# RWKV chunks of two decoder layers on one core: dense states, products on alternate halves, values' products ahead, norm by row tile

## Chip, cores and metric

One core of a Trainium2 chip runs the whole program. The metric is the device time of one execution in microseconds. TensorE's clock has two levels here, 2.4 GHz (granted clock 1.00 in the profile) and 1.2 GHz (0.50).

## Reference

Two stacks of two layers work on 256 tokens of 1024 features in float32. The change touches the second stack, whose layers `l` = 0, 1 each start with

```python
cols_a, cols_b, gate_a, gate_b = split_cols(h @ w_in[l], IN_SIZES)
y_a, v_first = rwkv7_branch(cols_a, ...)      # 8 heads of 64
y_b = dsa_branch(cols_b, ...)
merged = sigmoid(gate_a) * (y_a @ w_branch_a[l]) + sigmoid(gate_b) * (y_b @ w_branch_b[l])
x = x + merged @ w_out[l]
```

Within `rwkv7_branch` the state of a head, 64x64, runs over the tokens, and the output is normed by head:

```python
def step(state, inp):
    r_t, w_t, k_t, v_t, a_t, b_t = inp
    sa = jnp.einsum('bhvk,bhk->bhv', state, a_t)
    state = (state * w_t[:, :, None, :] + sa[..., None] * b_t[:, :, None, :]
             + v_t[..., None] * k_t[:, :, None, :])
    return state, jnp.einsum('bhvk,bhk->bhv', state, r_t)
...
y = (y - mean) * lax.rsqrt(var + RWKV_LNX_EPS)              # mean, var over the 64 of a head
y = y * lnx_g + lnx_b + bonus * v                           # bonus: one number per token and head
return y * g
```

## The kernel before

The program is written engine by engine, each with its own order of instructions; semaphores hand work over. A row tile `m` is 128 tokens (two of them). Weights come in pieces of 1 MB through a ring of five slots, issued by SyncE in the order in which they are planned; a piece waits until the one five places earlier has been used.

The recurrence is done in four chunks `c` of 64 tokens, `m, half = divmod(c, 2)`: a chunk lies in one half of the 128 partitions of its row tile. `solve_tensor` inverts the chunks' triangular matrices by doubling (`products`, L1893, 64x64 matmuls that alternate between the two halves of the partitions), and ends with VectorE's eviction of `("Y", l, g, 5)` into `self.solve`. Before it, L1884 forms the pair products in all four quarters (rows by columns) of the array.

Then `chunks_tensor` (all its products have line L1985) does for each chunk:
- the right side: 8 products of `packed[..., 1, :]` with the values, and for `c` > 0 4 products with the carried state, 128 rows deep: the state of two heads is one 128x128 block with zeros outside its two diagonal blocks (`zeros_gpsimd` writes the zeros);
- VectorE copies it to `self.rhs` (L2043);
- the output's first part: 8 products with the values, 4 with the carried state;
- the new state: 4 products of keys with values (64 rows deep, 128 wide), each followed for `c` > 0 by a product of the identity with the carried state, 128x128;
- `self.solve` times the right side, 8 products; ScalarE copies the result to `self.sa` (L2032), for which TensorE waits;
- 4 products of `self.bh` with it into the state, which VectorE scales by the decay (L2049, one instruction for each half), and 8 products into the output, which ScalarE copies (L2034).

PSUM has eight banks of 512 columns; right side, sa, output and state alternate between two banks each.

After the chunks come, on TensorE: `gate_tensor(pe, l, 1, 1)`, the fourth gate projection (16 matmuls of 128x128 on 512 columns); `turn_tensor(ya_turn)`, eight transposes of the normed `y`; `merge_tensor`, branch products a, b for columns 0 to 511, then a, b for 512 to 1023. On VectorE: `finish_vector` (L2060 to L2086, the norm over both row tiles at once, with a power on GpSimd, L506), the copy of the turned `y`, and `merge_vector`.

A float32 matmul leaves two records in the trace.

## Time and profile before

| | us |
|---|---|
| median of 3 runs | 3280.16 (3278.95 to 3289.49) |
| the profiled execution | 3287.36 |
| its span | 3285.6 |
| TensorE busy | 3075.7 (94% of the span) |
| VectorE busy | 1504.1 (46%) |
| ScalarE busy | 1029.3 (31%) |
| GpSimd busy | 108.3 (3%) |

The page gives the busy share of the engines and the granted clock in 40 slices, so a slice is 82 us. Views of the trace give single stretches in microseconds from the start of the span. In them PE is TensorE, PEld its weight load, DVE VectorE, ACT ScalarE, POOL GpSimd, SP SyncE, and what stands in brackets is the idle time before an instruction and what ended it.

### The profile page before, as it was taken

How to read it: one execution, taken by the hardware profiler on the slowest of the kernel's cores; microseconds unless marked ns; L12 is line 12 of the kernel's file. 1: busy time of each engine (PE TensorE's matmuls, PEld its weight loads, DVE VectorE, ACT ScalarE, POOL GpSimd, SP SyncE). 2: the span in 40 equal slices, each digit the busy share in tenths (PEclk: the TensorE clock that was granted, in tenths of full speed). 3: DMA queues.
4: the chain of work that ended last, by engine and by line, in shares of the span. 5: the costliest groups of instructions: out<-in, count | busy, mean ns of one | idle time of the engine just before them, and what ended most of it. 6: DMA issues, size and time to landing. Idle time of an engine off the chain costs nothing.

```text
span 3285.6 us, 35140 instructions
## 1 busy us (share of the span) xinstructions
PE 3075.7 (94%) x15248; PEld 2287.2 (70%) x15248; DVE 1504.1 (46%) x1739; ACT 1029.3 (31%) x1200; POOL 108.3 (3%) x105
## 2 busy tenths in 40 slices
PE   7996999999999999898799999978999999999999
PEld 6874567878785768744574588536746888888887
DVE  3455235454545154425723544267235444454444
ACT  3442124434342234203101343131013334334343
POOL 0001000000011000000100000001000000000000
PEclk9998999999999999998869999989699999999999
DMA  7541335556541535433204355432043455555554
GB/s 263 179 164 52 114 119 183 175 177 216 182 162 52 172 135 193 158 128 120 66 26 142 128 192 184 150 103 66 26 143 127 163 192 187 184 175 183 189 183 137
DMA packets 226582, 483.73 MB, mean 147 GB/s; under 512 B 11678, under 2 KB 45086, under 8 KB 225982
## 3 DMA queue, kind: packets, MB, share of 16 engines
q1 hardware_dynamic: 226048, 477.83, 43.1%
q10 hardware_dynamic: 380, 3.66, 0.4%
q8 instruction: 120, 1.97, 0.3%
q14 instruction: 34, 0.28, 0.0%
HBM read 476.75 MB, written 2.95 MB: 146 GB/s over the span
## 4 chain that ended last, share of the span: by engine, by line
PE 82%; DVE 9%; DMA 4%; ACT 2%; issue 1%; POOL 1%; SPq 0%; ACTq 0%; DVEq 0%; POOLq 0%
PE psum L354 19%; PE psum L351 17%; PE psum L353 17%; PE psum L352 17%; PE psum L1985 3%; PE psum L1893 2%; PE psum L715 2%; PE psum L690 1%; PE psum L472 1%; PE psum L557 1%; DMA weight_ring<-in_moe_wd 1%; PE psum L700 1%; ACT weight_high_halves L340 1%; DVE stage_area_halves L463 1%; DMA weight_ring<-in_ffn_w_gate 1%
## 5 line engine op out<-in xcount | busy, mean ns | idle before, releaser
L346 DVE TENSOR_TENSOR weight_ring_low_halves<-weight_ring,weight_high_halves 128x2048 fp32r<-128x2048 f32 (+1 forms) x346 | 741.7, 2151 | 879.7 <-ACT weight_high_halves L340 879.7
L351 PE MATMUL psum<-weight_high_halves,stage_area_halves 128*128 128x512 f32 (+2 forms) x2616 | 1008.1, 385 | 50.4 <-DVE stage_area_halves L463 36.0
L353 PE MATMUL psum<-weight_high_halves,stage_area_halves 128*128 128x512 f32 (+2 forms) x2616 | 998.2, 382 | 0.0
L352 PE MATMUL psum<-weight_ring_low_halves,stage_area_halves 128*128 128x512 f32 (+2 forms) x2616 | 997.6, 381 | 0.0
L340 ACT ACTIVATE weight_high_halves<-weight_ring 128x2048 fp32r<-128x2048 f32 (+1 forms) x346 | 622.4, 1806 | 794.3 <-PE psum L353 374.6
L354 PE MATMUL psum<-weight_ring,stage_area 128*128 128x512 f32 (+2 forms) x1600 | 671.4, 580 | 9.3 <-issue 6.7
L351 PEld LDWEIGHTS psum<-weight_high_halves,stage_area_halves 128*128 128x128 f32 x2616 | 495.3, 189 | 150.5 <-DVE stage_area_halves L463 26.3
L353 PEld LDWEIGHTS psum<-weight_high_halves,stage_area_halves 128*128 128x128 f32 x2616 | 494.9, 189 | 98.9
L352 PEld LDWEIGHTS psum<-weight_ring_low_halves,stage_area_halves 128*128 128x128 f32 x2616 | 494.4, 189 | 93.1
L354 PEld LDWEIGHTS psum<-weight_ring,stage_area 128*128 128x128 f32 x1600 | 303.6, 192 | 360.7 <-issue 355.6
L453 ACT ACTIVATE stage_area<-psum 128x512 f32<-128x512 f32 (+2 forms) x126 | 72.0, 579 | 608.9 <-PE psum L354 359.6
L460 ACT ACTIVATE stage_area_halves<-psum 128x512 fp32r<-128x512 f32 (+2 forms) x148 | 78.0, 571 | 218.3 <-PE psum L557 137.9
L506 POOL TENSOR_TENSOR small<-small,constants 128x1 f32<-128x1 f32 (+5 forms) x45 | 61.5, 1367 | 2272.0 <-DVE small L858 1213.3
L463 DVE TENSOR_TENSOR stage_area_halves<-psum,stage_area_halves 128x512 fp32r<-128x512 f32 (+2 forms) x148 | 90.4, 650 | 84.2 <-ACT stage_area_halves L460 83.1
L1985 PE MATMUL psum<-stage_area 64*64 64x64 f32 (+2 forms) x704 | 102.1, 332 | 7.1 <-ACT stage_area L2032 5.4
L690 PE MATMUL psum<-stage_area 64*128 64x256 f32 (+1 forms) x288 | 83.0, 436 | 25.2 <-DVE stage_area L745 14.3
L454 DVE COPY stage_area<-psum 128x512 f32<-128x512 f32 (+1 forms) x42 | 28.5, 678 | 165.7 <-PE psum L472 165.4
L1985 PEld LDWEIGHTS psum<-stage_area 64*64 64x64 f32 (+2 forms) x704 | 88.5, 219 | 19.4 <-issue 10.8
L615 ACT ACTIVATE stage_area<-psum 128x512 f32<-128x512 f32 (+2 forms) x108 | 59.6, 555 | 122.4 <-PE psum L353 122.3
L690 PEld LDWEIGHTS psum<-stage_area 64*128 64x128 f32 (+1 forms) x288 | 52.3, 207 | 53.1 <-issue 23.8
L472 PE MATMUL psum<-constants,stage_area 128*128 128x128 f32 x272 | 39.1, 302 | 50.8 <-ACT stage_area L1736 23.7
L715 PE MATMUL psum<-stage_area 128*64 128x256 f32 (+1 forms) x288 | 81.2, 420 | 0.0
(227 smaller groups left out, 1958.4 us busy)
## 6 DMA issues: line engine op xcount, KB each, us to landing
weight_ring<-in_ffn_w_down SPq DMA_DIRECT2D x44, 1024.0 KB, 5.0
weight_ring<-in_ffn_w_gate SPq DMA_DIRECT2D x40, 1024.0 KB, 5.2
weight_ring<-in_ffn_w_up SPq DMA_DIRECT2D x40, 1024.0 KB, 5.2
weight_ring<-in_moe_wd SPq DMA_DIRECT2D x40, 1024.0 KB, 4.9
weight_ring<-in_w_in SPq DMA_DIRECT2D x36, 1024.0 KB, 4.9
weight_ring<-in_moe_wg SPq DMA_DIRECT2D x32, 1024.0 KB, 5.2
weight_ring<-in_moe_wu SPq DMA_DIRECT2D x32, 1024.0 KB, 5.3
weight_ring<-in_mem_w_kv SPq DMA_DIRECT2D x16, 1024.0 KB, 5.1
```

What stands on the lines that cost most here:

```text
L340: act.raw.activation(self.high_half(name), self.in_slot(name), ACT.Copy).then_inc(*act.mark("high_halves", ("high", name)))
L346: v.raw.tensor_tensor(self.low_half(name), self.in_slot(name), self.high_half(name), ALU.subtract).then_inc(*v.mark("low_halves", ("halves ...
L351: pe.raw.matmul(out, a[1], w[0], start=start, stop=False)
L352: pe.raw.matmul(out, a[0], w[1], start=False, stop=False)
L353: return pe.raw.matmul(out, a[0], w[0], start=False, stop=stop)
L354: return pe.raw.matmul(out, a, w, start=start, stop=stop)
L453: return eng.raw.activation(dst, src, ACT.Copy)
L460: eng.raw.activation(dst[0], src, ACT.Copy).then_inc(*eng.mark("high_half_taken", (name, "high")))
L463: eng.raw.tensor_tensor(dst[1], src, dst[0], ALU.subtract).then_inc(*self.drained(eng, bank, full, name))
L690: mm = pe.raw.matmul(net.ps[:, bank, m * S:(m + 1) * S], h["q"](j, m), h["k"](j), start=(j == 0), stop=(j == h["nk"] - 1))
L715: mm = pe.raw.matmul(net.ps[p0:p0 + rows, bank, ct * S:(ct + 1) * S], h["v"](part, kt), net.pT[:, i % 2, kt, :], start=(kt == 0), stop=(kt ...
L1985: return pe.raw.matmul(net.ps[out_rows, bank, at], lhsT, rhs, start=start, stop=stop, skip_group_check=True)
```

## The change

- The states are dense: 64 columns for each head, two heads on the two halves of the partitions. A product with a carried state is 64 rows deep, eight instead of four, alternating between the heads of a pair (`e`). The zeroing on GpSimd goes. The identity product is one, on 256 columns.
- Even and odd heads' right sides and outputs lie in two banks each (0, 1 and 4, 5), with both row tiles in one bank; VectorE copies the even ones and ScalarE the odd ones. sa has bank 2, the state bank 3.
- The products of the values for all four chunks, and the state's for chunk 0, stand ahead of the wait for the solve's end.
- Two terms of the norm's end, `y_gain` = g x lnx_g and `y_bias` = (bonus x v + lnx_b) x g, are made by GpSimd; VectorE norms row tile by row tile, with two instructions at the end in place of five.
- The order after the fourth gate is b branch for both column halves, the turn of `y`, then the a branch row tile by row tile; the branch weights are loaded in the order b, b, a, a.

The removed lines of `chunks_tensor`, `finish_vector` and the merge are in the functions printed above; lines left out are marked.

```diff
-        self.state = [net.part(9216, 4, P), net.part(9728, 4, P)]
+        self.state = [net.part(9216, 4, CH), net.part(9728, 4, CH)]
+        self.y_gain, self.y_bias = (net.ax_buf[:, at:at + D].rearrange("p (m n) -> p m n", m=MT) for at in (0, D))
...
-            st["merge"] = []
-            for nb in range(2):
-                c0 = nb * BANK
...
+            branch = {}
+            for j in (1, 0):
+                for nb in range(2):
+                    w = ins[f"w_branch_{'ab'[j]}_2"][l]
+                    branch[nb, j] = net.plan_proj(f"branch{l}{'ab'[j]}{nb}", w[:, nb * BANK:(nb + 1) * BANK], [(0, BANK)], 4)
+            st["merge"] = [(branch[nb, 0], branch[nb, 1]) for nb in range(2)]
...
-    def zeros_gpsimd(self, pool, l):
-
...
     def chunks_tensor(self, pe, l):
-        pe.wait_ge(*pe.at(("Y", l, 0, 5), ("Y", l, 1, 5), ("zeroed", l)))
+        half_rows = [slice(0, CH), slice(CH, P)]
+        RHS, SA, STATE, Y = (0, 1), 2, 3, (4, 5)
+
+        def rhs_at(rows, e, m, i):
+            return net.ps[rows, RHS[e], m * S + i * CH:m * S + i * CH + CH]
+
+        def y_at(rows, m, h):
+            at = m * S + h // 2 * CH
+            return net.ps[rows, Y[h % 2], at:at + CH]
+
+        def state_at(e, c, i):
+            at = (c % 2) * S + i * CH
+            return net.ps[half_rows[e], STATE, at:at + CH]
+
+        def mm(out, lhsT, rhs, start=False, stop=False):
+            return pe.raw.matmul(out, lhsT, rhs, start=start, stop=stop, skip_group_check=True)
+
+        def rhs_values(m):
+            for i in range(4):
+                for e in range(2):
+                    h = 2 * i + e
+                    for rows in half_rows:
+                        x = mm(rhs_at(rows, e, m, i), self.packed[rows, 8 * m + h, 1, :], self.v[rows, m, h * CH:h * CH + CH], m == 0 and i == 0)
+                    if m == 1 and i == 3:
+                        x.then_inc(*net.full(pe, RHS[e], ("rhs", l, 0, e)))
+
+        def y_values(m):
+            for h in range(8):
+                for rows in half_rows:
+                    mm(y_at(rows, m, h), self.packed[rows, 8 * m + h, 2, :], self.v[rows, m, h * CH:h * CH + CH], m == 0 and h < 2)
+
+        def state_values(c):
+            m, half = divmod(c, 2)
+            rows = half_rows[half]
+            for i in range(4):
+                for e in range(2):
+                    h = 2 * i + e
+                    mm(state_at(e, c, i), self.k[rows, m, h * CH:h * CH + CH], self.v[rows, m, h * CH:h * CH + CH], i == 0)
+
+        for bank in RHS:
+            pe.wait_ge(*net.free(bank))
+        rhs_values(0)
+        rhs_values(1)
+        pe.wait_ge(*net.free(STATE))
+        state_values(0)
+        for bank in Y:
+            pe.wait_ge(*net.free(bank))
+        y_values(0)
+        y_values(1)
+        pe.wait_ge(*pe.at(("Y", l, 0, 5), ("Y", l, 1, 5)))
         for c in range(4):
             m, half = divmod(c, 2)
...
+            rows, state = half_rows[half], self.state[c % 2]
+            tokens = [slice(part * P + CH * half, part * P + CH * half + CH) for part in range(2)]
             if c:
                 pe.wait_ge(*pe.at(("state", l, c)))
...
+                for i in range(4):
+                    for e in range(2):
+                        x = mm(rhs_at(rows, e, m, i), self.arT[half_rows[e], i, m, tokens[0]], state[half_rows[e], i, :])
+                        if i == 3:
+                            x.then_inc(*net.full(pe, RHS[e], ("rhs", l, c, e)))
+                if c < 3:
+                    state_values(c)
+                    mm(net.ps[:, STATE, (c % 2) * S:(c % 2) * S + S], net.ident, state.rearrange("p i d -> p (i d)"))
+                for i in range(4):
+                    for e in range(2):
+                        if c == 2 and i == 0:
+                            pe.wait_ge(*net.free(Y[e]))
+                        mm(y_at(rows, m, 2 * i + e), self.arT[half_rows[e], i, m, tokens[1]], state[half_rows[e], i, :])
+            pe.wait_ge(*net.free(SA))
+            for e in range(2):
+                pe.wait_ge(*pe.at(("rhs_kept", l, c, e)))
+                for i in range(4):
+                    h = 2 * i + e
+                    x = mm(net.ps[rows, SA, h * CH:h * CH + CH], self.solve[rows, 8 * m + h, :], self.rhs[rows, half, h * CH:h * CH + CH], True, True)
+            x.then_inc(*net.full(pe, SA, ("sa", l, c)))
+            pe.wait_ge(*pe.at(("sa_kept", l, c)))
+            if c < 3:
+                for i in range(4):
+                    for e in range(2):
+                        h = 2 * i + e
+                        x = mm(state_at(e, c, i), self.bh[rows, m, h * CH:h * CH + CH], self.sa[rows, half, h * CH:h * CH + CH], False, True)
+                x.then_inc(*net.full(pe, STATE, ("new_state", l, c)))
             for h in range(8):
...
+                x = mm(y_at(rows, m, h), self.packed[rows, 8 * m + h, 0, :], self.sa[rows, half, h * CH:h * CH + CH], False, True)
+                if half and h >= 6:
+                    x.then_inc(*net.full(pe, Y[h % 2], ("y", l, m, h % 2)))
+
+    def rhs_keep(self, eng, l, c, e):
+        m, half = divmod(c, 2)
+        rows = slice(CH * half, CH * half + CH)
+        dst = self.rhs[rows, half, :].rearrange("p (i e d) -> p i e d", i=4, e=2)[:, :, e, :]
+        src = self.net.ps[rows, e, m * S:m * S + S].rearrange("p (i d) -> p i d", i=4)
+        return self.net.copy(eng, dst, src)
+
+    def y_keep(self, eng, m, e):
+        dst = self.y[:, m, :].rearrange("p (i e d) -> p i e d", i=4, e=2)[:, :, e, :]
+        src = self.net.ps[:, 4 + e, m * S:m * S + S].rearrange("p (i d) -> p i d", i=4)
+        return self.net.copy(eng, dst, src)
...
+            self.rhs_keep(act, l, c, 1).then_inc(*net.drained(act, 1, ("rhs", l, c, 1), ("rhs_kept", l, c, 1)))
...
+            if half:
+                act.wait_ge(*act.at(("y", l, m, 1)))
+                self.y_keep(act, m, 1).then_inc(*net.drained(act, 5, ("y", l, m, 1), ("y_kept", l, m, 1)))
...
             if c < 3:
...
+                src = net.ps[:, 3, (c % 2) * S:(c % 2) * S + S].rearrange("p (i d) -> p i d", i=4)
+                v.raw.tensor_tensor(self.state[(c + 1) % 2], src, widen(self.decay_end[:, :, c], 2, CH), ALU.mult).then_inc(
+                    *net.drained(v, 3, ("new_state", l, c), ("state", l, c + 1)))
+            if c == 1:
+                v.wait_ge(*v.at(("y", l, 0, 0)))
+                self.y_keep(v, 0, 0).then_inc(*net.drained(v, 4, ("y", l, 0, 0), ("y_kept", l, 0, 0)))
...
+    def finish_gpsimd(self, pool, l):
+
+        pool.wait_ge(*pool.at(("Y", l, 1, 5), ("rhs", l, 0, 1), ("g", l, 0), ("g", l, 1), ("loaded", ("vec", l, 7))))
+        row = lambda j: widen(self.vec[:, j, :], 1, MT)
+        by_head = lambda ap: ap.rearrange("p (h d) -> p h d", d=HD)
+        pool.raw.tensor_tensor(self.y_gain, self.g, row(6), ALU.mult)
+        for m in range(MT):
+            inst = pool.raw.tensor_tensor(by_head(self.y_bias[:, m, :]), by_head(self.v[:, m, :]), widen(self.bonus[:, m, :], 2, HD), ALU.mult)
+        inst.then_inc(*pool.step())
+        pool.wait_ge(*pool.last)
+        pool.raw.tensor_tensor(self.y_bias, self.y_bias, row(7), ALU.add).then_inc(*pool.step())
+        pool.wait_ge(*pool.last)
+        pool.raw.tensor_tensor(self.y_bias, self.y_bias, self.g, ALU.mult).then_inc(*pool.mark("finish_terms", ("finish_terms", l)))
...
     def finish_vector(self, v, l):
...
+        for m in range(MT):
+            y, tmp = self.y[:, m, :], self.at[:, m, :]
...
+            if m == 1:
+                v.wait_ge(*v.at(("y", l, 1, 0)))
+                self.y_keep(v, 1, 0).then_inc(*self.net.drained(v, 4, ("y", l, 1, 0), ("y_kept", l, 1, 0)))
+            v.wait_ge(*v.at(("y_kept", l, m, 0), ("y_kept", l, m, 1)))
+            v.raw.tensor_reduce(mean, heads(y), AX, ALU.add).then_inc(*v.step())
...
+            v.raw.tensor_scalar(var, var, 1.0 / HD, LNX_EPS, ALU.mult, ALU.add).then_inc(*v.mark("variance_ready", ("var", ("lnx", l, m))))
+            v.wait_ge(*v.at(("rstd", ("lnx", l, m))))
+            v.raw.tensor_tensor(heads(y), heads(y), widen(rstd, 2, HD), ALU.mult).then_inc(*v.step())
+            v.wait_ge(*v.last)
+            v.wait_ge(*v.at(("finish_terms", l)))
+            v.raw.tensor_tensor(y, y, self.y_gain[:, m, :], ALU.mult).then_inc(*v.step())
+            v.wait_ge(*v.last)
+            v.raw.tensor_tensor(y, y, self.y_bias[:, m, :], ALU.add).then_inc(*v.mark("rwkv_done", ("ya", l, m)))
...
     def merge_tensor(self, pe, l):
         net = self.net
...
+        for nb in range(2):
+            net.proj_tensor(pe, self.layers[l]["merge"][nb][1], lambda k, m: self.ybT[:, k, m * P:(m + 1) * P], lambda b, m: (6, 2)[nb] + m)
+        net.turn_tensor(pe, self.ya_turn(l))
+        for m in range(MT):
+            for nb in range(2):
+                tag, bank = self.layers[l]["merge"][nb][0]["tag"], (4, 0)[nb] + m
+                pe.wait_ge(*net.free(bank))
+                pe.wait_ge(*pe.at(("yaT", l, m)))
+                w = net.weights(pe, (tag, 0, 0))
+                for k in range(4):
+                    mm = net.product(pe, net.ps[:, bank, :], self.yaT[:, k, m * P:(m + 1) * P], at_k(w, k), k == 0, k == 3)
+                used = [("used", (tag, 0, 0))] if m == MT - 1 else []
+                mm.then_inc(*net.full(pe, bank, (tag, "full", 0, m), *used))
...
     def merge_vector(self, v, l):
         net = self.net
...
+        for nb in range(2):
+            tag, cols = self.layers[l]["merge"][nb][1]["tag"], slice(nb * BANK, (nb + 1) * BANK)
             for m in range(MT):
+                gb, bank = self.gate[1][:, m, cols], (6, 2)[nb] + m
+                v.wait_ge(*v.at((tag, "full", 0, m), ("gate", l, nb, 1, m)))
+                v.raw.tensor_tensor(gb, net.ps[:, bank, :], gb, ALU.mult).then_inc(*net.drained(v, bank, (tag, "full", 0, m), ("gb", l, nb, m)))
+        for m in range(MT):
+            for nb in range(2):
+                tag, cols, bank = self.layers[l]["merge"][nb][0]["tag"], slice(nb * BANK, (nb + 1) * BANK), (4, 0)[nb] + m
                 out = self.merged[:, m, cols]
+                v.wait_ge(*v.at((tag, "full", 0, m), ("gate", l, nb, 0, m)))
+                v.raw.tensor_tensor(out, net.ps[:, bank, :], self.gate[0][:, m, cols], ALU.mult).then_inc(*net.drained(v, bank, (tag, "full", 0, m), ("ga", l, nb, m)))
                 v.wait_ge(*v.at(("gb", l, nb, m), ("ga", l, nb, m)))
-                v.raw.tensor_tensor(out, out, gb, ALU.add).then_inc(*v.mark("branches_merged", *([("merged", l, m)] if nb == 1 else []), *([("groups_done", l)] if nb == 1 and m == 1 else [])))
+                v.raw.tensor_tensor(out, out, self.gate[1][:, m, cols], ALU.add).then_inc(*v.mark(
+                    "branches_merged", *([("merged", l, m)] if nb == 1 else []), *([("groups_done", l)] if nb == 1 and m == 1 else [])))
...
             self.gate_tensor(pe, l, 1, 1)
-            net.turn_tensor(pe, self.ya_turn(l))
             self.merge_tensor(pe, l)
...
             self.solve_gpsimd(pool, l)
-            self.zeros_gpsimd(pool, l)
-            rstd(("lnx", l), 16, 16)
+            self.finish_gpsimd(pool, l)
+            for m in range(MT):
+                rstd(("lnx", l, m), 16 + 8 * m, 8)
```

## Rows read from the trace of the kernel before

**Rows 1.** The page: granted clock of TensorE in 40 slices, in tenths.
```profile
PEclk9998999999999999998869999989699999999999
```

**Rows 2.** The chain that ended last, around the chunks: start, us, what.
```profile
1644.64 4.22 PE psum L1985 x56
1649.52 18.39 PE psum L1985 x104
1668.58 18.69 PE psum L1985 x104
...
1703.47 16.15 PE psum L354 x32
```

**Rows 3.** Windows: stretch, us, busy time by engine, granted clock, DMA share, GB/s.
```profile
1630.00:1644.00 14.00, 13.80 (x466) 13.66 (x462) 10.07 (x16) 0.00 (x0) 0.00 (x0) 1.00 0.02 4
...
1654.00:1660.00 6.00, 6.00 (x37) 5.24 (x36) 0.69 (x1) 0.00 (x0) 0.00 (x0) 0.50 0.00 0
1643.60:1703.40 59.80, 56.23 (x376) 48.17 (x370) 5.98 (x11) 4.14 (x7) 0.00 (x0) 0.55 0.00 1
2299.35:2359.46 60.11, 56.55 (x376) 48.48 (x371) 5.98 (x11) 4.14 (x7) 0.00 (x0) 0.55 0.00 1
...
1703.40:1719.40 16.00, 16.00 (x33) 6.83 (x32) 12.58 (x13) 1.19 (x2) 3.28 (x1) 0.86 0.13 38
```

**Rows 4.** Timeline of TensorE: start, us, line, tile rows*columns, moving operand, records.
```profile
1607.42 1.98 PE L1884 MATMUL psum<-stage_area 64*64 64x128 f32 x64 [0.78 <-ACT stage_area L453]
...
1641.69 1.10 PE L1893 MATMUL psum<-stage_area 64*64 64x64 f32 x32
1642.65 1.15 PE L1893 MATMUL psum<-scaled_residual 64*64 64x64 f32 x32
...
1644.64 2.05 PE L1985 MATMUL psum<-stage_area 64*64 64x64 f32 x32 [0.84 <-issue]
...
1660.87 0.79 PE L1985 MATMUL psum<-stage_area,constants 128*128 128x128 f32 x2
1661.59 0.79 PE L1985 MATMUL psum<-stage_area 64*128 64x128 f32 x2
...
1665.93 1.97 PE L1985 MATMUL psum<-stage_area 64*64 64x64 f32 x16
...
1720.98 27.70 PE L354 MATMUL psum<-weight_ring,stage_area 128*128 128x512 f32 x64 [0.46 <-issue]
```

**Rows 5.** Timeline of all engines: the hand-overs of the solve's end and chunk 0.
```profile
1641.90 0.69 DVE L1939 TENSOR_TENSOR scaled_residual<-psum,constants 128x512 f32<-128x512 f32 x1 [0.32 <-PE psum L1893]
...
1643.85 0.69 DVE L1951 TENSOR_TENSOR stage_area<-psum,scaled_residual 128x512 f32<-128x512 f32 x1 [0.32 <-PE psum L1893]
...
1644.64 4.20 PE L1985 MATMUL psum<-stage_area 64*64 64x64 f32 x56 [0.84 <-issue]
...
1648.88 0.59 ACT L2032 ACTIVATE stage_area<-psum 64x512 f32<-64x512 f32 x1 [41.60 <-PE psum L1985]
1649.52 1.47 PEld L1985 LDWEIGHTS psum<-stage_area 64*128 64x128 f32 x8 [0.82 <-ACT stage_area L2032]
...
1651.33 0.86 DVE L2049 TENSOR_TENSOR stage_area<-psum,small 64x256 f32<-64x256 f32 x2 [4.79 <-PE psum L1985]
```

**Rows 6.** The norm's end: timeline at the turn, then groups by shape (busy, mean ns).
```profile
1719.42 0.86 PEld L472 LDWEIGHTS psum<-constants,stage_area 128*128 128x128 f32 x8 [0.63 <-DVE stage_area L2086]
...
L2073 DVE TENSOR_TENSOR stage_area<-stage_area,small 128x512 f32<-128x512 f32 x2 | 1.3, 693 | 0.0
...
L506 POOL TENSOR_TENSOR small<-small,constants 128x8 f32<-128x8 f32 x4 | 6.6, 1646 | 52.5 <-DVE small L1517 52.5
```

**Rows 7.** Groups of POOL by shape, two-input operations on wide operands.
```profile
L1958 POOL TENSOR_TENSOR stage_area<-stage_area,constants 128x512 f32<-128x512 f32 x2 | 2.5, 1272 | 48.3 <-DVE stage_area L1928 48.3
...
L893 POOL TENSOR_TENSOR stage_area<-stage_area,constants 128x640 f32<-128x640 f32 x1 | 2.1, 2103 | 0.0
```

**Rows 8.** Timeline of SyncE: issues of branch weights before and in the fourth gate.
```profile
1603.18 0.37 SPq L310 DMA_DIRECT2D weight_ring<-in_w_branch_a  x1
1716.22 0.37 SPq L310 DMA_DIRECT2D weight_ring<-in_w_branch_b  x1
```

129 lines of the change are left out of this document (18 added, 111 removed).

## The prediction

> **What bounds the kernel now.** I read the page first, then the chain that ended last in order of time, then windows, then timelines. The clock row of the page [rows 1] stands near full speed except around slices 20 and 28, the chunk stages of layers 0 and 1. The chain [rows 2] runs there on TensorE's L1985 products alone, from 1644.64 to the gate projection at 1703.4, so TensorE sets the end. The windows [rows 3] say why the stage is long: from the last product of the solve to the gate it takes 59.8 us in layer 0 and 60.11 us in layer 1, TensorE busy for 56 of them at a mean granted clock of 0.55; 1654 to 1660 has it busy without a break at 0.50, the 1.2 GHz level. The solve just before, also of 64x64 products, holds 1.00 (2.4 GHz). The difference is in the form: the solve alternates between the two halves of the partitions, the chunk stage gives one half after another.
>
> The timelines [rows 4] give prices. A product is two records. At full clock:
> - Alternate halves: 32 records start every 0.96 us (1641.69, 1642.65), so 0.12 us per two products, 0.48 per eight.
> - One half: 32 records in 2.05 less a tail of 0.22, so 0.118 per product, 0.945 per eight.
> - All four quarters of the array: L1884, whose moving operand is 128 wide, has 64 records in 1.98 us, about 0.028 per record. One after another, a record twice as wide would take twice 0.059; two at a time would give 0.059, and it's half of that. So products in the same rows but other columns overlap too.
>
> At the low clock eight products in one half take 1.97 less a tail of 0.2, 1.77 us (1665.93). There the values' and identity products alternate every 0.72 us (1660.87, 1661.59). A dense record of 512 columns takes 27.70 / 64 = 0.43 us at full clock, so a product of 128 columns (two records) takes 0.22, and 0.43 at the low clock: about 0.29 is lost at each change between 64x128 and 128x128 tiles.
>
> **The change, part by part.** Counts per layer.
>
> *Values ahead.* 32 right-side, 8 state and 32 output products of values no longer wait for the solve's last eviction: 36 pairs x 0.12 = 4.3 us, and they start at once where 0.84 us of idle stood before 1644.64 [rows 5]. VectorE's last eviction (1643.85, 0.69) lies under them, and so do the first right-side copies.
>
> *Chunks.* Hand-overs [rows 5]: from the last solve-times-right-side product to the first product that reads ScalarE's copy 0.84 us is lost (the group of 56 ends at 1648.84, its last record began 0.22 before and would be followed 0.06 later; the next begins at 1649.52), 0.59 of it the copy. It stays in each chunk. VectorE starts 0.21 us after a last product is issued (1641.90 against the group whose successor starts at 1641.69), works 0.43 on 256 columns, and TensorE follows 0.10 later: 0.75 to 0.8.
> - Chunk 0: two groups in one half 1.89, one pair group 0.48, hand-over 0.84: 3.2 us. The state's scaling now takes one instruction of 256 columns (0.43) in place of two (0.86), and hides under the 0.945 us of output products.
> - Chunks 1 and 2: four pair groups 1.92 (carried state to right side, values to state, carried state to output, bh to state), two one-half groups 1.89, hand-over 0.84. One identity product of 256 columns takes 2 x 0.22 and two changes of tile form. No row shows such a change at full clock; its bounds are 0 and the low clock's 0.58 for both, and I take half, 0.3. Sum 5.4 us each, in place of 19.1 from hand-over to hand-over (1649.52 to 1668.58) [rows 2]. The split right-side copies (0.43 on VectorE, under 0.59 on ScalarE) and the output copy for which chunk 2 waits lie under 1.7 us of products.
> - Chunk 3: two pair groups 0.96, one-half groups 1.89, hand-over 0.84, and here only 0.48 covers the 0.76 of the right-side copies, so 0.28 is late: 4.0 us.
>
> Sum 4.3 + 3.2 + 10.8 + 4.0 = 22.3. Some 20 group starts whose weights aren't ahead add 0 to 0.05 each (the 0.96 already has one in 32 records); I take 0.7: **23.0 us**, bounds 21.7 (neither they nor the changes of form cost anything) and 24 (1.0, and the changes at 0.58). Gain 36.8 and 37.1 us.
>
> This takes 2.4 GHz throughout. It rests on rows: the new stage opens with 4.3 us of pairs, as in the solve; afterwards each chunk is thin around the hand-over, so it's also the weakest assumption.
>
> *Gate and merge.* From the gate's start to the first merge projection 17.58 us pass now (1703.40 to 1720.98): 0.86 mean clock over the gate [rows 3], 0.63 us of waiting for the norm [rows 6], then the turn, 1.5 with its copy (1719.42 to 1720.98) [rows 4, 6]. At full clock the gate's 32 records are half of the 27.70 row less its tail, 13.8 us; then the b branch's 32 run without waiting, 13.8, which is moved and not new, then the turn. So 17.6 becomes 15.3, **2.3 us** less per layer. The merge's last projection is still followed by one multiply and one add before its turn; the turn into bank 1 waits for the multiply, but the row tile 1 group already waits for the add, so that is hidden.
>
> *Norm by row tile.* Each tile has eight VectorE instructions of 512 columns (0.69 [rows 6]), two small ones and a POOL power of 8 columns (1.65): 7.5 us, the first tile starting before chunk 3 ends. Both are done 12 us after the stage; the turn needs them after 27.6 us (gate and b branch). If that cover were gone the 12 us would be paid. The copies of b's products into the gates come behind the turn on VectorE (4 x 0.69), but they hold banks 6, 7, 2, 3, which nobody needs until the merged turn.
>
> *POOL.* Four zeroings go; five tensor operations come, eight times 512 columns: 8 x 1.27 = 10.2 us by L1958 [rows 7], or 13.5 by the slower L893. They start 2.4 us into the stage and are wanted about 24 us in: hidden.
>
> *SP.* The branch pieces come as b, b, a, a. Three are loaded in the solve, the fourth once the gate has read its first piece, three quarters through (1603.18, 1716.22) [rows 8]; a's second is first read 18 us after the gate. Out's pieces follow b, b and a's first: b's come when the first two came, a's first about 4 us later than the old third, and the piece that waits for it is read 20 us later still. Cost nothing; its cover gone, one weight landing.
>
> **The sum.** 36.8 + 37.1 + 2 x 2.3 = 78.5 us off the profiled execution's own 3287.36 (its span 3285.6 and 1.8 around it): 3208.9. That execution stands 7.2 us above the runs' median of 3280.16, so the median is predicted at 3201.7, rounded to **3202**.
>
> **A rule weighed.** The row 1654 to 1660 has TensorE busy without a break and at half clock. The Trainium skill, TensorE: Matmul & The Clock Gate, "Loop structure matters more than you think", says that back-to-back matmuls stay warm; this trace disagrees for products in one half. By that rule alone the new stage stays at full clock, which is the sum above; by the row it may not, which is the first rival.
>
> **Rivals.**
> 1. *The clock falls inside the chunks.* For: the mean of 0.55 [rows 3] is 6 us at 1.00 and the rest at 0.50, so it fell in the first hand-over, after some 28 products mostly in one half; chunk 0 has as thin a stretch. Against: pairs precede and follow. At the low clock groups cost 0.96 and 1.77, the identity product 1.44: chunks 1 and 2 take 9.7 each, chunk 3 6.3, with 4.3 of values and 4.2 (between 3.2 and 5.3) for chunk 0 before: 34.2, and the gate's 2.3 goes too. A layer then gives 25.6 in place of 39.1: one layer 3216, both 3229.
> 2. *Halves don't overlap in the new tiles.* The carried-state and state products use the same columns or the same rows. 13 groups x 0.46 = 6.0 us per layer: 3214. L1884's four at once speak against.
> 3. *Two halves in one bank go singly.* The 64 values' products of prelude pairs would take 3.7 us more per layer: 3209. The solve's pairs share a bank and overlap [rows 4], so 1 in 100. The Trainium skill, TensorEngine Tiling, "Gotcha 1: PSUM Pressure", says that different row tiles cannot access the same PSUM bank at once; by that rule, 3209; the trace disagrees.
> 4. *Slower: POOL's terms come late.* VectorE stands in order at the wait for them, and ya, its turn and the drains stand behind. The turn is due 50 us in, and 9 us of norm follow the wait, so it starts to cost once POOL needs over 38 us for its 10.2, and decides once it passes 38 + 39 = 77 us, seven times the row; the slowest comparable row gives 13.5. Then over 3280; 1 in 100.
>
> **Chances.** Full clock through the chunks 0.62; rival 1 0.24 (one layer 0.14, both 0.10); rival 2 0.08; rival 3 0.01; rival 4 and anything else that eats it 0.02; no measurable change 0.01; the rest, 0.02, small extra waits. The likeliest one's own range is 3195 to 3209: twice the stage's bounds (3199 to 3204), widened by some 5 us to each side, half of what the runs of before lie apart (3278.95 to 3289.49). **3194 to 3231** reaches over rivals 1 to 3 and leaves out about 0.1. A change within 0.3%, 10 us, can't be told from none: faster 0.97, same 0.01, slower 0.02.
>
> **What would show it.** The granted clock at 1.00 from the solve through the gate; the stage 23 us; 64x64 records a few ns apart in pairs in the carried-state and state groups; one 128x128 product of 256 columns in chunks 1 and 2; ScalarE's sa copy followed by 0.1 us to TensorE; no wait before the ya turn; POOL's five operations over by mid-stage. Wrong: 0.50 in the stage, single spacing of 0.058 in the pair groups, a wait on VectorE's rhs or state instruction longer than 0.3 us, or TensorE idle at the turn.

## The result, and the profile after

The median of four runs fell from 3281.05 to **3206.95 us** (3196.75 to 3211.01), a ratio of 0.9765 with a 95% interval of 0.9736 to 0.9794; 3202 was forecast, within 3194 to 3231. The profiled execution took 3208.12 us with a span of 3206.3; its sum had been put at 3208.9. Of the page, the clock row answers to [rows 1]; the dents at the two chunk stages are gone, those that remain are elsewhere.

```profile
PEclk9998999999999999989899999988999999999999
```

The chain that ended last, around the chunks of layer 0 (start, us, what), answers to [rows 2]:

```profile
1640.99 5.14 PE psum L1980 x159
...
1646.15 0.60 ACT stage_area L2073
...
1646.80 4.56 PE psum L1980 x96
...
1651.38 0.60 ACT stage_area L2073
...
1657.24 1.91 PE psum L1980 x46
...
1659.17 0.44 DVE stage_area L454
...
1660.83 0.60 ACT stage_area L2073
...
1662.62 27.66 PE psum L354 x64
```

TensorE still holds the chain, but ScalarE's copy of sa now appears in it once per chunk, and VectorE's right-side copy once, in chunk 3. A chunk is 5.2 us long where one was 19.

In what follows the *stage* is the time from the solve's last product to the first one of the fourth gate, and the *merged turn* is the transpose of the merged branches, the first work that needs all of the merge. The windows of the stage in both layers, then the gate (columns as in [rows 3]; the five busy times are PE, PEld, DVE, ACT and POOL):

```profile
1640.77:1662.55 21.78, 19.01 (x461) 17.46 (x457) 6.84 (x14) 4.21 (x9) 9.05 (x5) 1.00 0.01 3
2258.41:2280.19 21.78, 19.01 (x460) 17.46 (x456) 6.83 (x14) 4.21 (x9) 9.05 (x5) 1.00 0.01 3
1662.55:1676.35 13.80, 13.80 (x34) 6.18 (x33) 7.98 (x15) 0.98 (x2) 3.29 (x2) 1.00 0.14 39
```

59.83 and 60.13 us became 21.78 twice, and the granted clock of both stages is 1.00 where it was 0.55. The timeline of the stage (engine, line, tile, moving operand, records):

```profile
1640.82 5.29 PE L1980 MATMUL psum<-stage_area 64*64 64x64 f32 x160
1641.04 0.69 DVE L1952 TENSOR_TENSOR stage_area<-psum,scaled_residual 128x512 f32<-128x512 f32 x1 [0.32 <-PE psum L1894]
1642.79 0.42 DVE L454 COPY stage_area<-psum 64x256 f32<-64x256 f32 x1 [1.06 <-PE psum L1980]
...
1643.00 2.35 POOL L2098 TENSOR_TENSOR scaled_residual<-stage_area 128x1024 f32<-128x1024 f32 x1 [29.57 <-PE psum L1980]
...
1646.15 0.59 ACT L2073 ACTIVATE stage_area<-psum 64x512 f32<-64x512 f32 x1 [2.87 <-PE psum L1980]
...
1646.80 2.37 PE L1980 MATMUL psum<-stage_area 64*64 64x64 f32 x64 [0.68 <-ACT stage_area L2073]
...
1649.09 0.70 PE L1980 MATMUL psum<-stage_area,constants 128*128 128x256 f32 x2
...
1649.72 1.61 PE L1980 MATMUL psum<-stage_area 64*64 64x64 f32 x32
1649.86 2.35 POOL L2105 TENSOR_TENSOR scaled_residual<-scaled_residual,stage_area 128x1024 f32<-128x1024 f32 x1
...
1652.02 2.37 PE L1980 MATMUL psum<-stage_area 64*64 64x64 f32 x64 [0.68 <-ACT stage_area L2073]
...
1659.65 1.00 PEld L1980 LDWEIGHTS psum<-stage_area 64*64 64x64 f32 x16 [0.18 <-DVE stage_area L454]
...
1661.47 1.14 PE L1980 MATMUL psum<-stage_area 64*64 64x64 f32 x16 [0.68 <-ACT stage_area L2073]
```

The values' products start 0.05 us behind the solve, with VectorE's last eviction lying beside them. From one hand-over to the next it is 5.22 us (1646.80, 1652.02), and the only idle time of TensorE left is 0.68 us before ScalarE's copy has landed, four times; in chunk 3 its weight loads also wait 0.18 us for the right-side copy. POOL works from 1643.00 to 1652.2.

At the turn (answers to [rows 6]):

```profile
1690.12 1.04 PE L472 MATMUL psum<-constants,stage_area 128*128 128x128 f32 x8
1691.55 1.95 PE L354 MATMUL psum<-weight_ring,stage_area 128*128 128x512 f32 x4 [0.39 <-issue]
```

The transposes follow the b branch without waiting; VectorE's norm had ended at 1674.45, 11.9 us after the stage.

Where the 79.24 us between the two profiled executions lie: 38.05 and 38.35 in the stages; 2.81 ahead of the first one, in code that is the same (1643.58 and 1640.77 from the start, with 129.7 and 126.3 us of low clock, of which the 3.4 us less can make 1.7 at most); and 0.03 in all the rest. The 2.24 us per layer at the merge don't show in the end, to which I come back.

### The profile page after: what moved, and what is told of

Its sections match the earlier page's. It is cut to its first block, busy times and chain, and to the rows that moved or that the text cites. A ratio compares the mean times of both kernels' runs of the same rounds, so it can differ in the third digit from the quotient of the medians.

```text
span 3206.3 us, 35492 instructions
## 1 busy us (share of the span) xinstructions
PE 2995.8 (93%) x15416; PEld 2224.0 (69%) x15416; DVE 1495.7 (47%) x1747; ACT 1029.0 (32%) x1204; POOL 124.1 (4%) x109
## 4 chain that ended last, share of the span: by engine, by line
PE 83%; DVE 9%; DMA 4%; ACT 2%; issue 1%; SPq 0%; POOL 0%; ACTq 0%; DVEq 0%; POOLq 0%
PE psum L354 20%; PE psum L351 18%; PE psum L353 17%; PE psum L352 17%; PE psum L1894 2%; PE psum L715 2%; PE psum L690 1%; PE psum L472 1%; DMA weight_ring<-in_moe_wd 1%; PE psum L1980 1%; PE psum L557 1%; PE psum L700 1%; ACT weight_high_halves L340 1%; DVE stage_area_halves L463 1%; DMA weight_ring<-in_ffn_w_gate 1%
## 5 line engine op out<-in xcount | busy, mean ns | idle before, releaser
L453 ACT ACTIVATE stage_area<-psum 128x512 f32<-128x512 f32 (+3 forms) x138 | 76.4, 561 | 699.5 <-PE psum L354 360.0
L454 DVE COPY stage_area<-psum 128x512 f32<-128x512 f32 (+2 forms) x54 | 33.5, 621 | 203.4 <-PE psum L472 196.9
L690 PE MATMUL psum<-stage_area 64*128 64x256 f32 (+1 forms) x288 | 82.9, 435 | 25.2 <-DVE stage_area L745 14.3
L615 ACT ACTIVATE stage_area<-psum 128x512 f32<-128x512 f32 (+2 forms) x108 | 59.5, 554 | 120.9 <-PE psum L353 120.8
L690 PEld LDWEIGHTS psum<-stage_area 64*128 64x128 f32 (+1 forms) x288 | 52.1, 207 | 52.9 <-issue 23.7
L472 PEld LDWEIGHTS psum<-constants,stage_area 128*128 128x128 f32 x272 | 35.0, 156 | 61.2 <-ACT stage_area L1737 25.6
L351 PE MATMUL psum<-stage_area_halves,weight_ring_low_halves 128*128 128x256 f32 x256 | 72.8, 285 | 4.7 <-DVE stage_area_halves L463 4.7
```

The lines of the kernel that those rows point to most:

```text
L351: pe.raw.matmul(out, a[1], w[0], start=start, stop=False)
L453: return eng.raw.activation(dst, src, ACT.Copy)
L472: mm = pe.raw.transpose(self.ps[:, g["bank"], i * P:(i + 1) * P], block, self.ident)
L690: mm = pe.raw.matmul(net.ps[:, bank, m * S:(m + 1) * S], h["q"](j, m), h["k"](j), start=(j == 0), stop=(j == h["nk"] - 1))
```

## Experiments

### Which part holds the clock

**All groups one half after another.** Same products and waits, the halves no longer alternate.

```diff
-            for i in range(4):
-                for e in range(2):
-                    ...
-                    for rows in half_rows:
-                        x = mm(rhs_at(rows, e, m, i), ...)
+            for rows in half_rows:
+                for i, e in ((i, e) for i in range(4) for e in range(2)):
+                        x = mm(rhs_at(rows, e, m, i), ...)
...
-                for i in range(4):
-                    for e in range(2):
+                for e in range(2):
+                    for i in range(4):
```

(the first hunk in both sets of values' products, the second in the state, carried-state and bh groups)

> The changed kernel with each group's two halves given one after the other: the same products and the same waits, but no product has one of the other half for its neighbour. My theory (the alternation of halves holds the granted clock and gives the overlap): the first 4 to 6 us still run at 1.00, then the clock falls to 0.50 as it did in the kernel before, and the stage takes 50 to 56 us in place of 21.8 (all at the low clock: 72 values' products x 0.221 = 15.9, chunk 0 6.2, chunks 1 and 2 12.9 each, chunk 3 8.2), so some 60 us more in all, 3270. Rival (what holds the clock is that the products stand close together, with few waits): clock 1.00 throughout, only the overlap is lost, 36 pairs x 0.116 = 4.2 and eleven chunk groups x 0.46 = 5.1, the stage 31 us, in all 3225.

3232.49 us, one run. Windows of layer 0 up to the clock's fall and from it to the gate, and of layer 1's stage:

```profile
1640.01:1649.86 9.85, 9.17 (x198) 9.03 (x195) 1.53 (x3) 0.97 (x2) 6.23 (x4) 1.00 0.01 3
1649.86:1676.68 26.82, 24.78 (x266) 22.56 (x263) 5.87 (x14) 3.29 (x7) 4.45 (x3) 0.50 0.01 1
2268.61:2301.15 32.54, 29.82 (x461) 27.88 (x457) 7.40 (x16) 4.26 (x9) 10.70 (x6) 0.75 0.01 2
```

The theory is right in kind and too dark in size: the clock falls to 0.50, but only 9.85 and 16.1 us into the stage, which takes 36.7 and 32.5 us. The rival's clock of 1.00 throughout is out.

**Only the chunks' groups so ordered** (the second hunk alone).

> The changed kernel with the values' products in alternate halves as they are, and only the chunks' groups (first state, carried state to right side and output, values to state, bh to state) given one half after another. With every group so given the clock fell 9.8 and 16.1 us into the stage; with only the values' so given it held. Theory (what loses the clock is a stretch whose products are nearly all in one half, with the hand-overs between): it falls here too, 5 to 10 us into the stage, and the stage takes 28 to 35 us with 12 us or more at 0.50. Rival (the stage's 4.3 us of pairs at its start are enough to hold it): 1.00 throughout and 21.8 + 11 groups x at most 0.46 = 24 to 26.9 us.

3231.82 us, one run:

```profile
1639.15:1652.07 12.92, 11.56 (x280) 10.88 (x276) 1.96 (x4) 1.94 (x4) 9.05 (x5) 1.00 0.01 3
1639.15:1670.10 30.95, 28.23 (x460) 26.29 (x456) 7.39 (x16) 4.26 (x9) 10.70 (x6) 0.71 0.01 2
2265.06:2299.03 33.97, 31.25 (x461) 28.89 (x457) 7.40 (x16) 4.26 (x9) 10.68 (x6) 0.62 0.01 2
```

The fall comes 12.9 and 8.2 us in, for 18.0 and 25.7 us. The alternation in the chunks is worth 9.2 and 12.2 us of stage, most of it clock; the pairs that open the stage don't hold the clock by themselves.

**Only the values' products so ordered** (the first hunk, and the same in `y_values`).

> The changed kernel with only the values' products ahead of the stage given one half after another; the state, carried-state and bh groups stay pairs. If the clock holds: 21.8 + 32 x 0.116 = 25.5 us at 1.00. If it is the one-half order ahead of the chunks that loses the clock (it fell 10 to 16 us into the stage where all groups were so given, and 6 to 7 us in where the values stood in the chunks): low from some 8 to 15 us on, 30 to 37 us.

3201.82 us, one run:

```profile
1634.93:1659.01 24.08, 21.31 (x461) 19.75 (x457) 6.84 (x14) 4.21 (x9) 9.04 (x5) 1.00 0.01 3
```

The clock holds through the stage in both layers (in layer 0 it falls behind it, see below), and the price is 2.30 us, not 3.7: the first group takes 7.59 us in place of 5.29. Its records start 58 ns apart inside a half, but some 6 ns apart for a few records where the order goes from one half to the other, so a short run of eight products is partly overlapped with the next.

**Values' products back in the chunks, in one half.**

```diff
-        rhs_values(0)
-        rhs_values(1)
+        rhs_values(0)                      # chunk 0's half alone
...
-        y_values(0)
-        y_values(1)
+        y_values(0)
...
+            if c < 3:
+                rhs_values(c + 1)
+                y_values(c + 1)
             pe.wait_ge(*net.free(SA))
```

> The changed kernel with the values' products back in the chunks, in one half: only chunk 0's 24 stand ahead, and each chunk gives the right-side and output values' products of the next one (16, in its half) before its own solve products. The other groups stay pairs, the states dense. My theory (the 72 products ahead are paid for only by the overlap they gain; the chunks' pair groups hold the clock): if the clock stays at 1.00 the stage is 21.8 + 32 pairs x 0.116 = 3.7, less 0.3 in chunk 3, whose late right-side copy is now covered: 25.2 us. Rival (a chunk with more one-half products than pairs loses the clock): 0.50 from chunk 0 or 1 on, about 24 one-half and 16 pair products per chunk, the stage 42 to 45 us (29.9 us for the chunks at the low clock's prices, 64 x 0.221 = 14.1 for the values, 1.0 for the first state's).

3239.68 us, one run:

```profile
1639.16:1644.95 5.79, 5.11 (x108) 4.97 (x106) 1.11 (x2) 0.97 (x2) 4.43 (x4) 1.00 0.01 3
1644.95:1674.73 29.78, 27.74 (x356) 25.62 (x356) 6.07 (x13) 3.29 (x7) 4.61 (x2) 0.54 0.01 2
2269.63:2305.71 36.08, 33.36 (x461) 31.00 (x457) 7.18 (x15) 4.26 (x9) 10.35 (x6) 0.59 0.01 2
```

My theory's 25.2 us at full clock is wrong. The rival's forecast holds in kind (a fall 5.8 us into the stage, 6.8 in layer 1), its 42 to 45 us are too many. The same 64 products given one half after another hold the clock when they all stand ahead in one piece, and lose it with 48 of them moved into the chunks: 14 us per layer, of which at most 3.7 are overlap. Why is open. In layer 0 the fall comes 0.13 us behind the first hand-over, before chunk 1, where the stage had given 48 products, all but the 8 of the state in one-half order (4.93 us), and a wait; with all 64 ahead it had given 80, again all but 8 in that order (7.59 us), and the same wait, and held. So what later chunks look like can't have brought this fall, and no run gives the values' products in the chunks and yet in alternate halves.

### How near the stage is to losing it

**Longer hand-overs.** ScalarE copies sa three times, then six times.

```diff
+            for _ in range(2):             # second kernel: range(5)
+                act.raw.activation(self.sa[rows, half, :], net.ps[rows, 2, :], ACT.Copy).then_inc(*act.step())
+                act.wait_ge(*act.last)
             act.raw.activation(self.sa[rows, half, :], net.ps[rows, 2, :], ACT.Copy)...
```

> The changed kernel with ScalarE's copy of the solve products done three times in a row, so that TensorE waits 0.68 + 2 x 0.6 = 1.9 us at each of the four hand-overs in place of 0.68. It asks how near the new stage is to losing the clock by its waits. If waits alone of this size don't matter: 1.00 throughout, the stage 21.8 + 4 x 1.2 = 26.6 us. If the stage stands near the edge: the clock falls to 0.50 in the chunks, over 32 us.

> As the one before, with the copy done six times: TensorE waits 0.68 + 5 x 0.6 = 3.7 us at each hand-over, about as long as the chunk's products take. At 1.00 the stage would be 21.8 + 12 = 33.8 us. I expect the clock to fall here from the first or second hand-over on, as TensorE is idle for nearly half of the time: over 40 us. Rival (waits don't count, only what the products are): 33.8 us at 1.00.

3229.33 and 3261.1 us, one run each. TensorE's timeline in the first kernel:

```profile
1643.67 3.76 PE L1980 MATMUL psum<-stage_area 64*64 64x64 f32 x64 [1.93 <-ACT stage_area L2076]
...
1647.36 1.22 PE L1980 MATMUL psum<-stage_area,constants 128*128 128x256 f32 x2
...
1653.27 4.17 PE L1980 MATMUL psum<-stage_area 64*64 64x64 f32 x64 [1.93 <-ACT stage_area L2076]
```

its windows up to the clock's fall and over the stage:

```profile
1636.40:1644.19 7.79, 5.86 (x185) 5.73 (x181) 1.11 (x2) 2.15 (x4) 5.48 (x4) 1.00 0.02 4
1636.40:1671.87 35.47, 27.75 (x461) 25.45 (x457) 7.18 (x15) 9.01 (x17) 10.50 (x6) 0.66 0.01 2
```

and the stage of the second:

```profile
1651.40:1694.88 43.48, 28.27 (x460) 25.96 (x457) 9.36 (x19) 16.12 (x29) 10.68 (x6) 0.66 0.01 2
```

At waits of 1.93 us in place of 0.68 the clock falls right behind the first one, 7.8 us into the stage (9.4 in layer 1). The waits themselves cost 5.0 us; the stage grows by 13.7 and 12.4, to 35.5 and 34.2. The products and their order are those of the changed kernel, so waits count too, and the stage of the changed kernel stands within 1.25 us per hand-over of the edge. Six copies give 43.5 and 44.4 us, as expected.

Three other profiles bear on the margin. Their stages end at full clock, but the clock falls 0.3 to 0.4 us into the dense products of the gate and stays low for 3.4 us: in layer 0 of the kernel with the values' products in one half after another, in layer 0 of the one begun at the low clock (next), and in layer 1 of the one with the chunks alone (below), whose stage is the changed kernel's. The gate's 13.8 us from its start, first and last of these:

```profile
1659.01:1672.81 13.80, 13.80 (x30) 6.00 (x29) 7.99 (x15) 0.98 (x2) 3.29 (x2) 0.88 0.04 3
2273.87:2287.67 13.80, 13.80 (x30) 6.00 (x29) 11.07 (x13) 0.98 (x2) 3.28 (x1) 0.88 0.05 3
```

In the first two the merged turn comes 1.70 us later for it (44.51 us after the gate's start in place of 42.81). The other layer of each, and both profiles of the changed kernel, have the gate at full clock. As the third of these stages is the changed kernel's, 21.78 us with the same waits, an execution of the changed kernel may pay this too.

**The stage begun at the low clock.**

```diff
+        pe.wait_ge(*pe.at(("paused", l)))
         for bank in RHS:
...
+        for _ in range(8):                 # VectorE, ahead of its part in the chunks
+            inst = v.raw.tensor_reduce(self.hs[:, 0:2], self.v, AX, ALU.add)
...
+        v.raw.tensor_reduce(self.hs[:, 0:2], self.v, AX, ALU.add).then_inc(*v.mark("pause_over", ("paused", l)))
```

> The changed kernel with nine VectorE reductions of 1024 columns (about 10 us) between the solve and the chunks, for which TensorE waits, so that the stage begins at the low clock; it prices the first rival of the prediction. If a stage that begins low stays low, it takes 39.6 us from its first values' product to the gate (values 8.6, chunk 0 5.3, chunks 1 and 2 9.7 each, chunk 3 6.3), and the gate begins low too. If the values' pairs bring the clock back, it is about 8.6 + 17.5 = 26 us, and the values ahead are what warms the stage as well as what holds it.

3237.27 us, one run. Windows from the first values' product on:

```profile
1658.49:1661.65 3.16, 3.11 (x58) 3.12 (x60) 0.00 (x0) 0.00 (x0) 0.00 (x0) 0.50 0.02 5
1661.65:1681.71 20.06, 17.29 (x400) 15.74 (x396) 6.14 (x13) 4.21 (x9) 9.05 (x5) 1.00 0.01 2
2285.59:2309.25 23.66, 20.83 (x453) 19.29 (x453) 6.15 (x13) 4.21 (x9) 9.04 (x5) 0.91 0.01 3
```

3.16 us of pairs bring back 2.4 GHz (4.1 in layer 1), and it then holds to the gate: 23.2 and 23.7 us in place of 21.8. So the stage repairs a start at the low clock for under 2 us, less than the 26 us in all that I gave for this case.

### The tail and the merge

**The merge as before** (chunks and the norm by row tile as changed).

```diff
+            net.turn_tensor(pe, self.ya_turn(l))
             self.merge_tensor(pe, l)       # a, b, a, b again, weights in that order
```

> The changed kernel with the merge as before: ya's turn right behind the fourth gate, then a, b, a, b, and the weight pieces in that order; chunks and the norm by row tile stay. Prediction's reading (the 2.3 us come from the full clock in the gate and from the norm that is over in time, and the new order of the branches is only cover): both norm tiles end 12 us after the stage, under the gate's 13.8, so no wait at the turn, and the merged turn starts 42.9 us after the gate's start, as in the changed kernel (42.81): total the same within 0.1%. Rival (the new order itself saves): the merged turn 45.1 us after the gate's start, total 4.6 us more.

Ratio to before 0.9755 (0.9737 to 0.9772), median 3205.6. The timeline at its turn:

```profile
1672.55 1.04 PE L472 MATMUL psum<-constants,stage_area 128*128 128x128 f32 x8
...
1673.97 2.38 PE L354 MATMUL psum<-weight_ring,stage_area 128*128 128x512 f32 x5 [0.39 <-issue]
```

13.84 us after the gate's start TensorE turns without waiting, and the merged turn starts at 42.81 us, to 0.01 as with the new order. The order of the branches is worth nothing here.

**Chunks alone:** in addition the norm over both row tiles, with the five instructions of its end, as in the kernel before.

> The change's chunk part alone: chunks of the changed kernel, with norm, POOL terms, turn and merge as before. My theory: stage 21.8 us at 1.00; the norm over both tiles ends about 16.0 us after the stage, the gate's 13.8 us end first, and the turn waits 2.2 to 2.9 us, so the merged turn starts 45.1 us after the gate's start. 76.4 us less than before in the two stages. If what the gate and merge gain is given back later anyway (both profiles reach the end of the kernel the same time after the gate), the total equals the changed kernel's; if that was chance, it is 4.5 us (0.14%) longer. Rival (the new tail is what makes the stage short): stage over 23 us.

Ratio 0.977 (0.9745 to 0.9794), median 3212.64.

```profile
1672.62 1.23 DVE L2128 TENSOR_TENSOR stage_area<-stage_area 128x1024 f32<-128x1024 f32 x1
1673.90 0.86 PEld L472 LDWEIGHTS psum<-constants,stage_area 128*128 128x128 f32 x8 [2.64 <-DVE stage_area L2128]
1673.90 1.09 PE L472 MATMUL psum<-constants,stage_area 128*128 128x128 f32 x8 [1.82 <-DVE stage_area L2128]
```

The stage is 21.78 us; the turn waits 1.82 us for the norm and the merged turn starts at 44.91 us, 2.10 later than in the changed kernel and 0.21 earlier than before (45.12). So the gate's full clock by itself buys 0.2 us, because the norm becomes late; the shorter norm buys 2.1 on top of it. Layer 1 confirms it: 3.4 us of its gate ran at 1.2 GHz, and its merged turn starts at 44.91 as well, where with the norm by row tile the same stretch costs 1.70 us. In the total neither can be told: the three kernels' intervals overlap.

### Both kernels once more

> The changed kernel itself, for comparison on the same chip: stage 21.8 us in both layers at 1.00, about 3207. Its time between the gate of layer 0 and the solve's end of layer 1, and behind the gate of layer 1 (595.87 and 926.12 in its first profile, 595.93 and 926.09 before the change) says whether the 2.2 us that the gate and merge gain are always given back in the feed-forward parts (then 596 and 926 again) or whether that was where low-clock stretches fell (then they vary by some us).

Median 3200.74 us (3198.11 to 3203.55), ratio 0.9733 (0.9715 to 0.975), stages 21.78 us.

> The kernel before, profiled once more. Its stages 59.8 and 60.1 us, low for 53 to 54 of them. Behind the gate of layer 1 its first profile took 926.09 us, and seven profiles with new chunks took 924.2 to 927.2 though the merged turn came 2.24 us sooner in six of them. If the feed-forward part takes the gain back (TensorE waits there longer for weights), 926 again; if the first profile was a lucky one, 928 or more.

3284.68 us, one run; stages 60.01 and 58.22 us. The two layers answer differently.

*Layer 0.* From its gate to the end of layer 1's solve the changed kernel took 595.87 us at first and 590.16 now, the kernel before 595.93 and 592.56. In the first profile of the changed kernel a low-clock stretch fell 329.1 us behind the gate, into the end of the feed-forward part, which neither the kernel before nor the second profile has there: 1.9 us of the gain stood before it and nothing behind it. In the second profile the gain of 2.2 us still stands at 355 us behind the gate. Of seven profiles with the new chunks (the changed kernel's two, those with an older tail, with the values' products in one-half order, begun low, and with filled hand-overs) three have that stretch and took 594.0 to 595.9 us, and four have not and took 590.0 to 592.4. Where it falls differs from one execution to the next, and what decides it is not shown.

*Layer 1.* Behind the gate it is 926.12 and 926.05 us with the change, 926.09 before, and 929.33 in its second profile, where a low-clock stretch 162 us behind the gate lasted 10.2 us and not 3.4. Windows of the expert layers, the same distances behind the gate; of before, of before again (second part only), and of the changed kernel:

```profile
2554.16:2919.46 365.30, 362.88 (x1708) 307.58 (x1707) 174.16 (x118) 145.94 (x116) 0.00 (x0) 1.00 0.55 183
2919.46:3281.46 362.00, 358.43 (x1686) 303.17 (x1684) 168.95 (x116) 139.60 (x112) 0.00 (x0) 1.00 0.52 173
```

```profile
2913.54:3275.54 362.00, 358.93 (x1690) 304.12 (x1690) 170.10 (x116) 141.49 (x113) 0.00 (x0) 1.00 0.52 175
```

```profile
2474.89:2840.19 365.30, 361.65 (x1703) 306.69 (x1702) 173.97 (x117) 146.59 (x117) 0.00 (x0) 1.00 0.54 181
2840.19:3202.19 362.00, 356.67 (x1681) 302.21 (x1679) 167.62 (x116) 138.80 (x112) 0.00 (x0) 1.00 0.52 173
```

TensorE is idle there for 5.99 us before and 8.98 with the change (5.92 and 8.30 in the second profiles): arriving 2.24 us sooner, it waits 2.4 to 3.0 us more between the experts' products. It waits for ScalarE's activation, which stands in order behind the splitting of the experts' weights, and that in part waits for their landing; ScalarE's waits for landings grow only from 170.1 to 173.9 us in the first profiles. That the transfers take the gain back is possible and not shown: no run slowed or quickened them, and other profiles don't fit it. Over the same windows five more have 6.7 to 8.4 us of idle time, 7.55 of it in the kernel with the chunks alone, which arrived only 0.2 us sooner; and the kernel with the values' products in one-half order, which has the changed tail and a low-clock stretch of the same 3.4 us, took 924.25 us from layer 1's gate to the end, 1.84 less than before. So the gain was lost in both profiles of the changed kernel, and it need not be.

### Work put into the hand-overs

```diff
         y_values(0)
-        y_values(1)
...
                 if c < 3:
                     state_values(c)
-                    mm(net.ps[:, STATE, (c % 2) * S:(c % 2) * S + S], net.ident, state.rearrange("p i d -> p (i d)"))
...
             x.then_inc(*net.full(pe, SA, ("sa", l, c)))
+            if c == 0:
+                y_values(1)
+            elif c < 3:
+                mm(net.ps[:, STATE, (c % 2) * S:(c % 2) * S + S], net.ident, state.rearrange("p i d -> p (i d)"))
             pe.wait_ge(*pe.at(("sa_kept", l, c)))
```

> The changed kernel with work put into the hand-over around ScalarE's copy of the solve products (0.68 us of TensorE waiting, four times per layer): in chunk 0 the second row tile's 16 output values' products (0.96 us) stand behind the solve products in place of ahead of the stage, in chunks 1 and 2 the identity product (0.70). What stays ahead of the solve products, 0.96 us of pair groups, still covers the right-side copies (0.43 and 0.59, 0.76 with their starts). Theory: three of four waits of 0.68 go, the stage takes 21.78 - 2.04 = 19.7 us at 1.00, 4 us less in all (0.13%), which is within what runs of one kernel differ by. Rival (the identity product behind the solve products puts its change of tile form and its wait for the state's bank onto the path, or the right-side copies are no longer covered): the wait moves to the right-side copies or to bh's products, and the stage stays over 21 us.

```profile
1650.79:1670.13 19.34, 18.51 (x460) 17.23 (x456) 6.84 (x14) 4.21 (x9) 9.06 (x5) 1.00 0.02 3
2264.97:2284.32 19.35, 18.52 (x461) 17.23 (x457) 6.84 (x14) 4.21 (x9) 9.06 (x5) 1.00 0.01 3
```

and the one hand-over of layer 0 at which TensorE still waits, chunk 3's:

```profile
1669.06 1.14 PE L1980 MATMUL psum<-stage_area 64*64 64x64 f32 x16 [0.68 <-ACT stage_area L2075]
```

The stage takes 19.35 us in both layers, 2.43 less than in the changed kernel, a little more than the three waits of 0.68; the chunks are 4.45 us apart instead of 5.22, so a little of the change of tile form (from 64x64 to 128x128 and back) probably goes with the wait. In the total it doesn't show: 3202.79 us (0.9736, 0.9717 to 0.9754) against 3200.74 for the changed kernel on the same chip. It is the shortest stage of all. With one wait of 0.68 left in place of four it should also be the one farthest from the edge found above; no run lengthened its waits to show it.

## Why the prediction was right

*The stage, 23.0 us with bounds 21.7 to 24: measured 21.78 in both layers, close to the lower bound.* Term by term: values and chunk 0 were put at 7.5 us and took 7.45 (6.03 from 1640.77 to 1646.80, then one pair group and one one-half group, 1.42). Chunks 1 and 2: 5.4 each, measured 5.22. The identity product and its two changes of tile form were put at 0.73 and take 0.63 from its start to the next product's, with another 0.09 lost before its start: both changes cost 0.3, as taken from bounds of 0 and 0.58. Chunk 3: 4.0, measured 3.9, its late right-side copy 0.18 and not 0.28. The sa hand-over was 0.84 and is 0.85 by the same reckoning. The term that failed is the 0.7 for some 20 group starts: in sum it measures nothing. By the starts of the single records some do cost (the carried states' output group takes 0.52 us in place of 0.48, and the values-to-state group 0.62 with the 0.09 just named), but a one-half group followed by a pair group is overlapped with it, which the sum had not foreseen: chunk 0's outputs and chunk 1's right side take 1.16 us in place of 1.43. So 0.7 + 0.36 + 0.1 + 0.05 make up the 1.2, with errors that partly cancel.

*2.4 GHz throughout, the weakest assumption: held in all eight stages profiled with the changed chunk code as it is (the changed kernel twice, and the two with an older tail).* The gate held too in seven of the eight. The reason given was the 4.3 us of pairs that open the stage, and that was not it: in one-half order these products hold the clock as well, and as pairs they don't hold it over one-half chunks. That it held was a choice with 0.62 on it and not a derivation. The runs show three conditions, and each one taken away alone lost the clock in both layers of its one profile: pairs within the chunks (9 to 12 us without), the values' products out of the chunks (14 us), short hand-overs (12 to 14 us at 1.93, 5.0 of it the waits themselves). On the rule weighed: the Trainium skill, TensorE: Matmul & The Clock Gate, "Loop structure matters more than you think", says that matmuls issued back to back stay warm and long waits between them cool the engine. The longer hand-overs agree with its second half, with waits of only 1.93 us. With its first half the kernel before disagrees [rows 3], busy 6.00 of 6.00 us at 0.50. And at the same waits of 0.68, one-half order in the chunks alone loses the clock (0.71 and 0.62 over the stage), so how the products lie in the array counts beside how closely they follow each other.

*Rival 1* had 0.24 and didn't happen in the changed kernel; it is what happens in five of the variants. Its price, 34.2 us for the stage, is near what those took (31.0 to 36.7, without the one with six copies), but doesn't come from the same terms: they fell later and hold more waits or less overlap, so the nearness is in part luck. (One layer's price in the total is 3215, not 3216.)

*Rivals 2 and 3:* out. 160 records open the stage in 5.29 us; a carried-state group of eight products starts its records in pairs 6 ns apart. The Trainium skill, TensorEngine Tiling, "Gotcha 1: PSUM Pressure", has different row tiles unable to use one bank at once; the values' pairs write one bank from both halves, at 0.12 us a pair, so the trace disagrees again.

*Gate and merge, 2.3 us per layer: 2.31 measured at the merged turn's start, 2.24 at the first projection behind it,* but the step named two causes as a sum, the gate's clock and the end of the norm's wait, and they aren't independent. The 0.63 us read as waiting for the norm [rows 6] are the weight load's; the turn's products followed the gate's without a visible wait, because the slow gate (16.06 us) ended as late as the norm. So the full clock had 2.25 us to give, and without the shorter norm it gives 0.2. And the gain doesn't reach the end in either profile of the changed kernel that was compared from layer 1's gate on; that the later parts take it over unchanged was a step that I didn't argue at all.

*Norm, POOL, SP as hidden work: right.* Norm 7.2 us a tile (7.5), over 11.9 us after the stage (12 predicted); POOL 9.05 us, below the 10.2, and over at 1652.2, 13 us before VectorE asks for its terms, so nothing of rival 4; the fourth branch piece was issued at 1673.14, 17 us ahead of the turn.

*The total.* The sum gave 3208.9 for an execution like the profiled one, and 3208.12 came out, with errors that cancel: 2.5 too few for the stages, 2.8 too few ahead of them, which no row of before announced and of which the clock explains 1.7 at most, 4.6 too many for the merge. That the sum came within 0.8 us is luck. The shift by 7.2 us to the median was a property of that one execution of before; the median of after is 1.2 below its own profiled execution.

## What to carry to other kernels

Here products that keep one half of the partitions busy were a matter of clock before they were one of overlap: check the granted clock of a thin stage first, and of the dense stretch just behind it, alternate the halves, gather what depends on nothing at its front, and then look how much longer a hand-over may get before the clock goes. Filling hand-overs with work that is free of them shortens the stage even where the total can't show it, and may give distance from the edge. A gain of 2 us ahead of 900 us of other work must be followed to the end, in more than one profile, before it is counted.

## What the runs showed of the hardware

- A stage of 64x64 products in alternate halves fell to 1.2 GHz with a wait of 1.93 us at each hand-over and stayed at 2.4 with 0.68; begun at 1.2 it was back at 2.4 after 3.16 us of pairs (4.1 in layer 1).
- The same stage with waits of 0.68 fell to 1.2 GHz when its chunk groups were given one half after another (12.9 and 8.2 us in).
- Behind three of fourteen stages that ended at 2.4 GHz the clock fell 0.3 to 0.4 us into the dense 512-column products of the gate, for 3.4 us.
- Runs of eight one-half products overlap a little with the next run in the other half: 64 products cost 2.30 us more than in pairs where 3.7 were expected.
- A 128x128 product of 256 columns between 64x64 ones took 0.63 us from its start to the next start at full clock, and began 0.09 us late, where the columns alone are 0.43 by the 512-column row.
- The same code took 590.2 and 595.9 us between layer 0's gate and layer 1's solve in two executions of one kernel, with 44.5 and 44.4 us of low clock that lay in other places; that its place alone makes the difference is likely and not shown.
